# Attention keys projected turned, with their rotary on DVE and GpSimd and partner rows moved by DMA

## The chip, the cores and the metric

One core of a Trainium2 chip. The engines are PE (TensorE, matrix products), ACT (ScalarE), DVE (VectorE), POOL (GpSimd) and SP (it only issues DMAs here). The metric is the device time of one call of the whole layer in microseconds; lower is better.

## What is computed

One decoder layer over a sequence of 512 rows of width 1024, everything in fp32:

```python
u = rms_norm(h, norm_gain);  z = u @ w_in          # 512 x 4420 columns
q_a, k_a, v_a, g_a, q_i, k_i, w_i, q_r, k_r, v_r, g_r = split(z)
q_a, k_a, q_i, k_i = rotary(..., first 16 of 64 head dims, theta 500000)
score = sum_h w_i[t,h] * relu(q_i[t,h] . k_i[s]);  keep the top 128 causal keys
y_a = softmax(q_a k_a^T over the kept keys) v_a * silu(g_a)      # 8 heads x 64
y_r = retention(rotary(q_r), rotary(k_r), v_r) * silu(g_r)       # 4 heads
out = rms_norm(h + concat(y_a, y_r) @ w_out) * final_gain
```

The rotary turns head dims 0 to 7 against their partners 8 to 15: x1 cos - x2 sin and x2 cos + x1 sin. The other 48 dims of a head stay as they are.

## The kernel before, in words

Each fp32 operand of a projection is split into two fp32r parts: ACT writes the rounded part (`w_hi`, L736), DVE the rest (`w_lo`, L1150), and three products (hi·hi, lo·hi, hi·lo) stand for one. The weights come in units of 256 rows by 512 columns (512 KB), four units to a chunk of 512 columns. A unit lives in a ring of six split slots. The chunks are, in order: 0 index, 1 queries, 2 keys, 3 values, 4 retention q and k, 5 retention v, 6 attention gate, 7 retention gate, and then two chunks of `w_out`.

All engines walk through the same list of **slots** g. A chunk has four slots, one for each tile of 128 rows: slot 8 to 11 are the keys, 12 to 15 the values, 16 to 19 retention q/k. In slot g, PE computes 24 products of 512 columns for tile g (`proj`, L527 to L529), with some other work between the first twelve ("first half") and the last twelve ("second half"). Unit u of a chunk is wanted a quarter slot after the one before it; `proj` waits for its `w_lo` at each quarter. Chunk 6 is computed turned: the weights are stationary and 512 tokens move (L523 to L525). The other chunks have x stationary and give tokens by columns.

The order of each engine within a slot is written out by hand, and each engine runs its instructions strictly in order:

- Weight splits (`splits_at`, L143): in slot 4c the first unit of the next chunk, in 4c+1 the second, in 4c+3 the last two. Units 18 and 19, which the second half of slot 16 wants, are so split in slot 15, by ACT and then by DVE.
- Keys: in the slot's end ACT copies the product to `zt`, scaled by the rms factor (L791). POOL turns the first 16 dims of each head in place (L1087, L1088, L1091: five instructions a tile). Two slots later PE transposes the tile in four pieces (L547) into the bank `mid_ps`, ACT writes its rounded part to `k_stack` rows 0 to 63 (L826, two instructions) and DVE the rest to rows 64 to 127 (`key_lo`, L1224, two instructions, one input in PSUM and one in SBUF). Retention q/k (slots 16 to 19) go the same way, with a rotary over all dims.
- `turn_rstd` (PE, slot 15) turns the rms factors into a row for all partitions, `half_rstd_row`, which holds half of each factor.
- Index scores and top-k: in slots 6 to 8 DVE forms the scores of blocks 1 to 3 of 128 queries. Then each block takes 16 rounds of MAX8 (L1261) and MATCH_REPLACE8 (L1263) over 256, 384 or 512 columns, and a mask (L1267) after its last round. `rounds_at` (L175) says how many rounds DVE does at the end of each slot: 4 in slots 6 to 9, 3 in 10 to 15, then 2 until the 48 are done (slot 22).
- `block_q_lo(0)` (DVE, slot 13, L1234): four instructions on 64x512 that split the queries of block 0.
- Attention visits: `scores(0)` is at the end of slot 17 on PE and needs all of `k_stack` (`klo_done`). DVE adds the mask and takes the maxima (L1280), ACT takes exponentials (L866) and scales (L873), PE transposes at the end of slot 18 (L610). Blocks 1, 2 and 3 need their masks from slot 21, 24 and 28.
- POOL in slots 16 to 19: the retention rotary of each tile, which PE transposes two slots later.

Of the kernel before, what the change touches and what calls it, by code (L numbers as in the profile page):

```python
# [12 lines left out]
P = 128  # L13
# [39 lines left out]
LEFT = 5 * P  # L53
C_V, C_RQK, C_RV, C_AG, C_RG = 3, 4, 5, 6, 7
ATT0 = MT * C_RQK
# [65 lines left out]


def first_chunk(x, norm_gain, w_in):
# [51 lines left out]
def rounds_at(slot):  # L175

    done = 0
    for g in range(TOPK0, slot + 1):
        n = min(4 if g <= 9 else 3 if g <= 15 else 2, ROUNDS * (MT - 1) - done)
        done += n  # L180
    return range(done - n, done) if slot >= TOPK0 else range(0)


def transposed(g):

    c = g // MT
    if g < 0 or g >= GROUPS or c not in (0, 1, 2, C_RQK):
        return None
    return g if c < 3 else g - MT


def hymba_layer(nc, x, w_in, w_out, final_gain, table, first, out):
    with ExitStack() as ctx:
# [50 lines left out]
        mix = sb("mix", [P, MT, 2 * ATT_W])  # L244
        attT = mix[:, :, 0:ATT_W]
        first_in = [t[:, :, :].rearrange("p m c -> p (m c)") for t in (mix, x_h)]
        gain = first_in[0][:, 0:NORM]
# [32 lines left out]
        def sems(names):  # L280
# [26 lines left out]
            "idx_lo_done idx_mm relu_done score_step round_step mask_done")  # L307

        klo_done, q_hi_done, q_rest_done, q_lo_done, qk_done, max_done, negmax_done, exp_done = sems(
            "klo_done q_hi_done q_rest_done q_lo_done qk_done max_done negmax_done exp_done")  # L310
# [71 lines left out]
        def _(sp):  # L382
# [51 lines left out]
        def _(pe):  # L434
# [55 lines left out]
            def proj(g, q):  # L490
# [44 lines left out]
            def transpose_group(g):  # L535
# [4 lines left out]
                if i > MT:  # L540
                    pe.wait_ge(t_evac, i)
                if i == 3 * MT:
# [30 lines left out]
            def turn_rstd():  # L573

                pe.wait_ge(rstd_spread, 1)
                pe.wait_ge(t_evac, 3 * MT)
                pe.wait_ge(klo_done, MT)
                for m in range(MT):
# [107 lines left out]
            for g in range(MT, GROUPS + OUT_GROUPS):  # L686
# [37 lines left out]
        def _(act):  # L724
# [41 lines left out]
            def project_out(g):  # L766
# [19 lines left out]
                if i is not None:  # L786
                    if i >= MT + 2:
                        act.wait_ge(t_done, i - 1)
                    if i >= 3 * MT + 2:
                        act.wait_ge(kz_done, i - 3 * MT - 1)  # L790
                    act.activation(zt[:, g % 2, :], src[:, :], ACT.Copy, scale=scale).then_inc(z_done, 1)  # L791
                elif c in (C_V, C_RV):
                    dst = (v_att if c == C_V else v_ret)[:, m, :]
                    act.activation(dst, src[:, :], ACT.Copy, scale=scale).then_inc(z_done, 1)
                else:
                    i = g - MT * C_AG
                    if i > MT:
                        act.wait_ge(rgate_done, i - MT)
                    elif i:
                        act.wait_ge(agate_done, i)  # L800
                    else:
                        act.wait_ge(rope_done, 4 * MT)
                    if i < MT:
# [5 lines left out]
            def transposed_out(g):  # L809
# [6 lines left out]
                if c == 0:  # L816
# [6 lines left out]
                    return  # L823
                if c == 2:
                    for hh in range(2):
                        ins = act.activation(k_stack[0:64, hh::2, t], mid_ps[64 * hh:64 * hh + 64, :].rearrange(  # L826
                            "p (a t) -> p a t", a=PAIRS), ACT.Copy)
                    ins.then_inc(t_evac, 1)
                    return
                if i == 3 * MT:  # L830
                    act.wait_ge(idx_mm, IDX_HEADS * (MT - 1))
                src = mid_ps[:, :].rearrange("p (a t) -> p a t", a=4)
                dst = {1: qT, C_RQK: retT[:, 0:4, :]}[c][:, :, t]
                act.activation(dst, src, ACT.Copy).then_inc(t_evac, 1)

            def relus(b):
# [102 lines left out]
            for g in range(MT, GROUPS + OUT_GROUPS):  # L939
# [11 lines left out]
                if MT + 2 <= g <= 2 * MT:  # L951
                    relus(g - MT - 1)
                if g == ATT0 - 1:
                    rstd_row()
                if g < GROUPS:
                    project_out(g)
# [44 lines left out]
        def _(pool):  # L1001
            step = 0

            def xi_times_q(m):

                t = slice(m * P, (m + 1) * P)
                pool.wait_ge(t_evac, 3 * MT + m + 1)
                pool.tensor_tensor(qxT[:, :, t], qrT[:, :, t], T("xi").rearrange("p (a t) -> p a t", a=2),
# [45 lines left out]
            x_rstd(0)  # L1054
            x_rstd(1)

            for g in range(MT, GROUPS):
# [15 lines left out]
                if ret:  # L1073
                    pool.wait_ge(tab_in, 16)
                if i == 3 * MT:
                    pool.wait_ge(warmed, 1)
                    pool.wait_ge(hrstd_done, 2)
                    pool.tensor_copy(half_rstd_row[:, :].rearrange("p (m t) -> p m t", m=MT), half_rstd.rearrange(
                        "p (m t) -> p m t", t=1).broadcast_to([P, MT, P])).then_inc(rstd_spread, 1)
                zg = g + 1  # L1080
                pool.wait_ge(z_done, zg)
                pool.wait_ge(rope_done, i)
                for s in range(2):

                    if i == 4 * MT - 1 and s:
                        pool.wait_ge(q_lo_done, 2)
# [5 lines left out]
                add.then_inc(rope_done, 1)  # L1092
                if c in (1, 2):
                    continue
# [24 lines left out]
            pad_q(0)  # L1119
            pool.wait_ge(t_done, 4 * MT)  # L1120
            pool.memset(zt[:, :, :], 0.0).then_inc(state_zeroed, 1)
# [25 lines left out]
        def _(dve):  # L1147
# [70 lines left out]

            def key_lo(m):

                t = slice(m * P, (m + 1) * P)
                dve.wait_ge(t_evac, 2 * MT + m + 1)
                for hh in range(2):
                    ins = dve.tensor_tensor(k_stack[64:128, hh::2, t], mid_ps[64 * hh:64 * hh + 64, :].rearrange(  # L1224
                        "p (a t) -> p a t", a=PAIRS), k_stack[0:64, hh::2, t].bitcast(F32), ALU.subtract)
                ins.then_inc(klo_done, 1)

# [190 lines left out]
            for g in range(MT, GROUPS + OUT_GROUPS):  # L1418
# [66 lines left out]
```

## Time and the profile before

| | |
|---|---|
| time, median of 3 runs | 280.89 us (280.73 to 304.37) |
| the profiled execution, its own time | 280.87 us |
| its span in the profile | 279.1 us |
| around the span | 1.77 us |
| busy share: PE, DVE, ACT, POOL | 97%, 72%, 56%, 23% |

The span is the time from the first to the last instruction in the profile of one execution. Times in the rows below are microseconds from its start. The busy share of PE is an upper bound, as its products overlap in the record: how close it is to its limit is read from the distance between the starts of two products.

### The profile page before, as it was taken

The page shows a single profiled execution, that of the slowest core. Times are in us where ns is not written, and L with a number is a line of the kernel's source. Part 1 is how long each engine was busy: PE and PEld are TensorE (multiplying, and loading weights), DVE is VectorE, ACT ScalarE, POOL GpSimd, SP SyncE. Part 2 cuts the span into 40 slices and gives each one's busy share as a digit, 9 for nine tenths or more (in the row PEclk, how much of TensorE's full clock was granted, in tenths as well). Part 3 has the DMA queues.
Part 4 walks back from the last instruction along what each step waited for, and adds up shares of the span by engine and source line. Part 5 has one row for each costly group of instructions (what it writes and reads, how often), then busy time and mean ns, then how long its engine had stood idle before and what let it go on. Part 6 is the DMA issues. An engine that isn't in the chain of part 4 may idle for free.

```text
span 279.1 us, 4372 instructions
## 1 busy us (share of the span) xinstructions
PE 271.7 (97%) x1493; PEld 227.0 (81%) x1493; DVE 200.5 (72%) x419; ACT 157.2 (56%) x331; POOL 64.2 (23%) x116
## 2 busy tenths in 40 slices
PE   8999999999999999999999999999999999999992
PEld 8988888888878788787888888788788888888891
DVE  3786889999999997999696663685656825563342
ACT  4896755536455423767658646776675694241231
POOL 2036622322300059767300102103020020000211
PEclk9999999999999999999999999999999999999999
DMA  7999504220422045052204220040120275111223
GB/s 267 403 400 350 154 4 150 75 76 2 150 76 78 0 150 150 2 150 73 80 2 150 75 78 0 6 147 23 59 73 0 77 237 177 36 41 38 78 88 139
DMA packets 13989, 30.10 MB, mean 108 GB/s; under 512 B 1168, under 2 KB 1680, under 8 KB 13968
## 3 DMA queue, kind: packets, MB, share of 16 engines
q1 hardware_dynamic: 13392, 29.04, 31.2%
q10 hardware_dynamic: 576, 0.79, 0.7%
q8 instruction: 12, 0.20, 0.3%
q14 instruction: 9, 0.07, 0.1%
HBM read 27.73 MB, written 2.10 MB: 107 GB/s over the span
## 4 chain that ended last, share of the span: by engine, by line
PE 67%; DVE 24%; DMA 3%; issue 2%; ACT 2%; SPq 1%; POOLq 0%; DVEq 0%; ACTq 0%
PE bank L527 14%; PE bank L529 13%; PE bank L528 13%; DVE keys L1263 6%; DVE top L1261 6%; DVE w_lo L1150 5%; PE bank L594 4%; PE bank L610 3%; PE bank L523 3%; DMA x_h<-in_first 3%; PE bank L524 3%; PE bank L525 3%; DVE k_stack L1224 2%; PE bank L626 2%; PE bank L625 2%
## 5 line engine op out<-in xcount | busy, mean ns | idle before, releaser
L527 PE MATMUL bank<-w_hi,xT_hi 128*128 128x512 f32 (+1 forms) x264 | 104.2, 395 | 0.1
L529 PE MATMUL bank<-w_hi,xT_lo 128*128 128x512 f32 (+1 forms) x264 | 101.5, 384 | 0.0
L528 PE MATMUL bank<-w_lo,xT_hi 128*128 128x512 f32 (+1 forms) x264 | 101.2, 383 | 0.0
L529 PEld LDWEIGHTS bank<-w_hi,xT_lo 128*128 128x128 f32 x264 | 49.6, 188 | 10.2
L527 PEld LDWEIGHTS bank<-w_hi,xT_hi 128*128 128x128 f32 x264 | 49.7, 188 | 9.8 <-issue 0.7
L528 PEld LDWEIGHTS bank<-w_lo,xT_hi 128*128 128x128 f32 x264 | 49.7, 188 | 8.8
L1150 DVE TENSOR_TENSOR w_lo<-w_raw,w_hi 128x1024 fp32r<-128x1024 f32 x35 | 43.9, 1276 | 13.1 <-ACT w_hi L736 12.8
L736 ACT ACTIVATE w_hi<-w_raw 128x1024 fp32r<-128x1024 f32 x35 | 36.6, 1055 | 6.9 <-PE bank L529 5.0
L1261 DVE MAX8 top<-keys 128x8 f32<-128x256 f32 (+2 forms) x48 | 26.8, 558 | 1.3
L1087 POOL TENSOR_TENSOR th<-zt,tab 128x64 f32<-128x64 f32 (+1 forms) x24 | 12.8, 535 | 62.2 <-ACT zt L791 57.7
L1263 DVE MATCH_REPLACE8 keys<-top,keys 128x256 f32<-128x256 f32 (+2 forms) x48 | 26.0, 542 | 0.0
L791 ACT ACTIVATE zt<-bank,small 128x512 f32<-128x512 f32 x12 | 8.2, 686 | 19.9 <-PE bank L529 19.8
L1021 POOL TENSOR_SCALAR small<-small 128x4 f32<-128x4 f32 (+1 forms) x6 | 1.6, 272 | 57.6 <-ACT st_sb L907 57.1
L866 ACT ACTIVATE work<-work,small 128x128 f32<-128x128 f32 (+3 forms) x16 | 8.8, 554 | 10.2 <-DVE small L1284 10.2
L1400 DVE TENSOR_TENSOR retT<-bank,retT 128x512 f32<-128x512 f32 (+1 forms) x9 | 5.7, 630 | 11.8 <-PE bank L529 11.8
L989 ACT ACTIVATE st_sb<-retT 128x512 f32<-128x512 f32 (+1 forms) x8 | 4.8, 606 | 16.3 <-DVE retT L1400 16.3
L1088 POOL TENSOR_TENSOR tmp<-zt,tab 128x64 f32<-128x64 f32 (+1 forms) x24 | 13.5, 562 | 0.0
L523 PE MATMUL bank<-xT_hi,w_hi 128*128 128x512 f32 x32 | 13.2, 411 | 0.0
L524 PE MATMUL bank<-xT_hi,w_lo 128*128 128x512 f32 x32 | 12.6, 392 | 0.0
L525 PE MATMUL bank<-xT_lo,w_hi 128*128 128x512 f32 x32 | 12.5, 391 | 0.0
L866 ACT ACTIVATE prob_odd<-prob_odd,small 128x128 f32<-128x128 f32 (+3 forms) x16 | 8.8, 553 | 6.4 <-DVE small L1284 6.3
L1116 POOL COPY q_pad<-retT 64x256 f32<-64x256 f32 x8 | 4.3, 535 | 26.8 <-PE bank L635 26.4
(173 smaller groups left out, 442.2 us busy)
## 6 DMA issues: line engine op xcount, KB each, us to landing
w_raw<-in_w_in SPq DMA_DIRECT2D x27, 512.0 KB, 3.8
w_raw<-in_w_out SPq DMA_DIRECT2D x8, 512.0 KB, 3.6
retT<-in_x SPq DMA_DIRECT2D x8, 256.0 KB, 3.4
x_h<-in_first SPq DMA_DIRECT2D x2, 836.0 KB, 8.2
out<-x_h SPq DMA_DIRECT2D x4, 320.0 KB, 2.5
mix<-in_first SPq DMA_DIRECT2D x3, 418.0 KB, 5.3
v_ret<-in_x SPq DMA_DIRECT2D x2, 512.0 KB, 10.4
v_att<-in_x SPq DMA_DIRECT2D x2, 512.0 KB, 12.1
```

Of the source, the lines that this page charges most:

```text
L523: pe.matmul(o, hi[:, kk, e], xT_hi[:, k, :], start=first, stop=False)
L524: pe.matmul(o, lo[:, kk, e], xT_hi[:, k, :], start=False, stop=False)
L525: mm = pe.matmul(o, hi[:, kk, e], xT_lo[:, k, :], start=False, stop=last)
L527: pe.matmul(o, xh, hi[:, kk, c0:c0 + w], start=first, stop=False)
L528: pe.matmul(o, xh, lo[:, kk, c0:c0 + w], start=False, stop=False)
L529: mm = pe.matmul(o, xl, hi[:, kk, c0:c0 + w], start=False, stop=last)
L736: act.activation(split_unit(w_hi, u), raw_unit(u), ACT.Copy).then_inc(whi_done, 1)
L866: act.activation(pr, pr, ACT.Exp, bias=neg_max[:, i:i + 1], scale=HD ** -0.5, accum_out=den[:, b % 2, h:h + 1]).then_inc(exp_done, 1)
L1088: last = chain(pool.tensor_tensor(tb[:, :, s, :], z[:, :, 1 - s, :], sin[:, :, s, :].broadcast_to([P, heads, half]), ALU.mult))
L1150: dve.tensor_tensor(split_unit(w_lo, u), raw_unit(u), split_unit(w_hi, u).bitcast(F32), ALU.subtract).then_inc(wlo_done, 1)
L1261: dve.max(top8[:, :], keys[b][:, :]).then_inc(round_step, 1)
L1263: dve.match_replace(keys[b][:, :], top8[:, :], keys[b][:, :], TAKEN).then_inc(round_step, 1)
```

## The change

The key chunk is computed turned, as chunk 6 already is. ACT then copies each product, unscaled, to `keys_raw` (the storage of `v_ret`): partitions are two heads of 64 dims, columns are tokens. There are no transposes of the key tiles any more. The rotary is done once for all keys, on whole rows of 2048 columns (4 head pairs by 512 tokens):

- SP loads a new 512 KB table (cosines and signed sines by partition and token) into `prob_odd` after unit 10. POOL multiplies both halves by `half_rstd_row` (two instructions on 128x512). `turn_rstd` moves from slot 15 to slot 10 for that, and POOL's spreading of the factors to before its loop.
- Slot 12: ACT issues four DMAs that copy the 8-partition groups of `keys_raw` to their partners' places in `keys_swapped` (the storage of `retT`, 80 partitions by 2048 columns, zeroed by POOL before).
- POOL multiplies `keys_swapped` by the sines: one instruction on 80x2048.
- Slot 13: DVE multiplies `keys_raw` by the cosines, four instructions on 128x512, once the DMAs have landed.
- POOL adds `keys_swapped` to `keys_raw`: one instruction on 80x2048 (`key_roped`).
- Slots 15 and 16: ACT writes the rounded part (`key_hi`, two instructions on 64x1024 in each). Slots 16 and 17: DVE writes the rest (`key_lo`, likewise, now with both inputs in SBUF).
- `rounds_at`: 4 rounds in slots 6 to 8, 3 in 9 to 12, then 2 (until slot 24).

```diff
-        n = min(4 if g <= 9 else 3 if g <= 15 else 2, ROUNDS * (MT - 1) - done)
+        n = min(4 if g <= 8 else 3 if g <= 12 else 2, ROUNDS * (MT - 1) - done)
...
+                if u == APART + RAW:
+                    sp.wait_ge(wlo_done, APART + 1)
+                    sp.dma_start(prob_odd[:, :, :].rearrange("p a t -> p (a t)"), key_table).then_inc(key_table_in, 16)
...
-                    if c == C_AG:
+                    if c in (C_K, C_AG):
...
-                if 2 * MT < i <= 3 * MT:
-                    pe.wait_ge(klo_done, i - 2 * MT)
...
-                if g == ATT0 - 1:
+                if g == MT * C_K + 2:
                     turn_rstd()
...
+                elif c == C_K:
+                    if m == 0:
+                        act.wait_ge(sq_act, 3)
+                        act.wait_ge(sq_dve, 1)
+                    act.activation(keys_raw[:, m, :], src[:, :], ACT.Copy).then_inc(z_done, 1)
...
+            def swap_keys():
+
+                act.wait_ge(z_done, SWAP_AT)
+                act.wait_ge(swapped_zeroed, 1)
+                for hh in range(2):
+                    for x in range(2):
...
+                        act.dma_start(keys_swapped[to, :, :], keys_raw[of, :, :]).then_inc(swapped_in, 16)
+
+            def key_hi(hh):
+
+                act.wait_ge(key_roped, 1)
+                for half in range(2):
+                    act.activation(k_stack[0:64, hh + 4 * half:hh + 4 * half + 3:2, :],
+                                   keys_raw[64 * hh:64 * hh + 64, 2 * half:2 * half + 2, :], ACT.Copy).then_inc(khi_done, 1)
...
+            def rope_keys():
+
+                pool.wait_ge(key_table_in, 16)
+                pool.wait_ge(rstd_row_done, 1)
+                for t in (key_cos, key_sin):
+                    pool.tensor_tensor(t, t, half_rstd_row[:, :], ALU.mult).then_inc(key_table_done, 1)
+                pool.wait_ge(key_table_done, 2)
+                pool.wait_ge(idx_mm, IDX_HEADS * (MT - 1))
+                pool.memset(keys_swapped, 0.0).then_inc(swapped_zeroed, 1)
+                pool.wait_ge(swapped_in, 16 * 4)
+                sin = key_sin[0:TURNED, :].rearrange("p (a t) -> p a t", a=1).broadcast_to([TURNED, PAIRS, SEQ])
+                pool.tensor_tensor(keys_swapped, keys_swapped, sin, ALU.mult).then_inc(key_sined, 1)
+                pool.wait_ge(key_cosed, PAIRS)
+                pool.wait_ge(key_sined, 1)
+                z = keys_raw[0:TURNED, :, :]
+                pool.tensor_tensor(z, z, keys_swapped, ALU.add).then_inc(key_roped, 1)
...
+            def key_cosine():
+
+                dve.wait_ge(key_table_done, 1)
+                dve.wait_ge(swapped_in, 16 * 4)
+                for n in range(PAIRS):
+                    dve.tensor_tensor(keys_raw[:, n, :], keys_raw[:, n, :], key_cos, ALU.mult).then_inc(key_cosed, 1)
+
+            def key_lo(hh):
+
+                for half in range(2):
+                    heads = slice(hh + 4 * half, hh + 4 * half + 3, 2)
+                    dve.wait_ge(khi_done, 2 * hh + half + 1)
+                    dve.tensor_tensor(k_stack[64:128, heads, :], keys_raw[64 * hh:64 * hh + 64, 2 * half:2 * half + 2, :],
+                                      k_stack[0:64, heads, :].bitcast(F32), ALU.subtract).then_inc(klo_done, 1)
...
-                if 0 <= g - 2 - 2 * MT < MT:
-                    key_lo(g - 2 - 2 * MT)
+                if g == SWAP_AT + 1:
+                    key_cosine()
+                if g - SWAP_AT - 4 in (0, 1):
+                    key_lo(g - SWAP_AT - 4)
```

`SWAP_AT` is 12. `retT` is free for retention again once `key_roped` is there (ACT waits for it in slot 18).

## Rows read from the trace of the kernel before

**Rows 1.** The page: busy time by engine, and the granted clock in 40 slices

```profile
PE 271.7 (97%) x1493; PEld 227.0 (81%) x1493; DVE 200.5 (72%) x419; ACT 157.2 (56%) x331; POOL 64.2 (23%) x116
...
PEclk9999999999999999999999999999999999999999
```

**Rows 2.** Waits (engine, line, releaser: us, times, longest): PE on a split

```profile
PEld bank L527 <- DVE w_lo L1150: 0.5, 1, 0.5
```

**Rows 3.** Timeline of PE (start, us, line, xcount): slots 10, 11, 14, 15 begin

```profile
58.53 0.39 PE L527 MATMUL bank<-w_hi,xT_hi 128*128 128x512 f32 x1
...
64.44 0.39 PE L527 MATMUL bank<-w_hi,xT_hi 128*128 128x512 f32 x1
...
82.39 0.39 PE L527 MATMUL bank<-w_hi,xT_hi 128*128 128x512 f32 x1
...
87.83 0.39 PE L527 MATMUL bank<-w_hi,xT_hi 128*128 128x512 f32 x1
```

**Rows 4.** Timeline of PE: middle of slot 16, scores, end of slot 18

```profile
96.25 0.39 PE L529 MATMUL bank<-w_hi,xT_lo 128*128 128x512 f32 x1
96.73 0.50 PE L527 MATMUL bank<-w_hi,xT_hi 128*128 128x512 f32 x1
...
105.03 0.22 PE L625 MATMUL bank<-k_stack,q_hl 128*128 128x128 f32 x1
...
105.88 0.45 PE L527 MATMUL bank<-w_hi,xT_hi 128*128 128x512 f32 x1
...
111.68 0.39 PE L529 MATMUL bank<-w_hi,xT_lo 128*128 128x512 f32 x1
112.22 1.02 PE L610 MATMUL bank<-ident_t,work 128*128 128x128 f32 x4 [0.15 <-ACT work L873]
113.00 0.47 PE L527 MATMUL bank<-w_hi,xT_hi 128*128 128x512 f32 x1
```

**Rows 5.** Timeline of DVE: slot 10, slot 15

```profile
63.88 1.39 DVE L1224 TENSOR_TENSOR k_stack<-bank,k_stack 64x512 fp32r<-64x512 f32 x2
65.30 0.56 DVE L1261 MAX8 top<-keys 128x8 f32<-128x384 f32 x1
...
66.56 0.56 DVE L1261 MAX8 top<-keys 128x8 f32<-128x384 f32 x1
...
95.46 2.35 DVE L1150 TENSOR_TENSOR w_lo<-w_raw,w_hi 128x1024 fp32r<-128x1024 f32 x2
97.72 0.55 DVE L1261 MAX8 top<-keys 128x8 f32<-128x384 f32 x1
```

**Rows 6.** Timeline of ACT: splits of unit 15 and of slot 12

```profile
67.42 1.06 ACT L736 ACTIVATE w_hi<-w_raw 128x1024 fp32r<-128x1024 f32 x1 [0.30 <-PE bank L529]
...
71.16 1.05 ACT L736 ACTIVATE w_hi<-w_raw 128x1024 fp32r<-128x1024 f32 x1
```

**Rows 7.** ACT's line 997, a DMA issue: ns min/median/max, and its landing

```profile
L997 ACTq DMA_DIRECT2D out<-x_h x4: 338/346/376, 260.3 to 276.0; - x4
...
DMA to landing us min/median/max: 2.6/2.8/4.6
```

**Rows 8.** Timeline of POOL: retention rotary of slots 16 and 18

```profile
101.96 0.74 POOL L1087 TENSOR_TENSOR th<-zt,tab 128x256 f32<-128x256 f32 x1
102.66 1.72 POOL L1088 TENSOR_TENSOR tmp<-zt,tab 128x256 f32<-128x256 f32 x1
...
116.85 1.30 POOL L1091 TENSOR_TENSOR zt<-th,tmp 128x512 f32<-128x512 f32 x1
118.23 1.48 POOL L1097 TENSOR_TENSOR kz<-zt,tab 128x256 f32<-128x256 f32 x1
```

**Rows 9.** Timeline of DVE beside POOL: splits, and a round between them

```profile
102.15 1.64 DVE L1150 TENSOR_TENSOR w_lo<-w_raw,w_hi 128x1024 fp32r<-128x1024 f32 x1
103.71 0.68 DVE L1261 MAX8 top<-keys 128x8 f32<-128x512 f32 x1
...
117.29 3.49 DVE L1150 TENSOR_TENSOR w_lo<-w_raw,w_hi 128x1024 fp32r<-128x1024 f32 x2
```

More of the change, by code:

```diff
@@ L120, in tables, with key_tables @@
     return t
+def key_tables():
+    t = np.zeros((2, 2, HD, SEQ), np.float32)
+    inv = np.float32(1.0) / (np.float32(ROPE_THETA) ** (np.arange(ROPE_HALF, dtype=np.float32) / np.float32(ROPE_HALF)))
+    ang = (inv[:, None] * np.arange(SEQ, dtype=np.float32)[None, :]).astype(np.float32).astype(np.float64)
+    t[0] = 2.0
+    for x, sign in ((0, -2.0), (1, 2.0)):
+        t[0, :, x * ROPE_HALF:(x + 1) * ROPE_HALF] = 2.0 * np.cos(ang)
+        t[1, :, x * ROPE_HALF:(x + 1) * ROPE_HALF] = sign * np.sin(ang)
+    return np.ascontiguousarray(t.reshape(2, P, SEQ).transpose(1, 0, 2).reshape(P, 2 * SEQ))
 def first_chunk(x, norm_gain, w_in):
@@ L186, in transposed, with hymba_layer @@
     c = g // MT
-    if g < 0 or g >= GROUPS or c not in (0, 1, 2, C_RQK):
+    if g < 0 or g >= GROUPS or c not in (0, 1, C_RQK):
         return None
-    return g if c < 3 else g - MT
-def hymba_layer(nc, x, w_in, w_out, final_gain, table, first, out):
+    return g if c < 2 else g - 2 * MT
+def hymba_layer(nc, x, w_in, w_out, final_gain, table, first, key_table, out):
     with ExitStack() as ctx:
@@ L575, in turn_rstd @@
                 pe.wait_ge(rstd_spread, 1)
-                pe.wait_ge(t_evac, 3 * MT)
-                pe.wait_ge(klo_done, MT)
+                pe.wait_ge(t_evac, 2 * MT)
                 for m in range(MT):
@@ L788, in project_out @@
                         act.wait_ge(t_done, i - 1)
-                    if i >= 3 * MT + 2:
-                        act.wait_ge(kz_done, i - 3 * MT - 1)
+                    if i >= 2 * MT + 2:
+                        act.wait_ge(kz_done, i - 2 * MT - 1)
                     act.activation(zt[:, g % 2, :], src[:, :], ACT.Copy, scale=scale).then_inc(z_done, 1)
+                elif c == C_K:
[3 more added lines that the diff above has]
+                    act.activation(keys_raw[:, m, :], src[:, :], ACT.Copy).then_inc(z_done, 1)
                 elif c in (C_V, C_RV):
+                    if c == C_RV and m == 0:
+                        act.wait_ge(klo_done, 4)
                     dst = (v_att if c == C_V else v_ret)[:, m, :]
@@ L823, in transposed_out @@
                     return
[L824 to L831, printed above, removed]
+                if i == 2 * MT:
+                    act.wait_ge(key_roped, 1)
                 src = mid_ps[:, :].rearrange("p (a t) -> p a t", a=4)
@@ L834, in transposed_out @@
                 act.activation(dst, src, ACT.Copy).then_inc(t_evac, 1)
+            def swap_keys():
[3 more added lines that the diff above has]
+                    for x in range(2):
+                        here, there = rope_halves(x)
+                        to = slice(HD * hh + here.start, HD * hh + here.stop)
+                        of = slice(HD * hh + there.start, HD * hh + there.stop)
+                        act.dma_start(keys_swapped[to, :, :], keys_raw[of, :, :]).then_inc(swapped_in, 16)
+            def key_hi(hh):
+                act.wait_ge(key_roped, 1)
+                for half in range(2):
+                    act.activation(k_stack[0:64, hh + 4 * half:hh + 4 * half + 3:2, :],
+                                   keys_raw[64 * hh:64 * hh + 64, 2 * half:2 * half + 2, :], ACT.Copy).then_inc(khi_done, 1)
             def relus(b):
@@ L952, in _ @@
                     relus(g - MT - 1)
-                if g == ATT0 - 1:
+                if g == MT * C_K + 2:
                     rstd_row()
+                if g == SWAP_AT:
+                    swap_keys()
+                if g - SWAP_AT - 3 in (0, 1):
+                    key_hi(g - SWAP_AT - 3)
                 if g < GROUPS:
@@ L1083, in _ @@
                 for s in range(2):
-                    if i == 4 * MT - 1 and s:
+                    if i == 3 * MT - 1 and s:
                         pool.wait_ge(q_lo_done, 2)
```

40 lines of the change are left out of this document (21 added, 19 removed).

## The prediction

> **What bounds the kernel now.** I read the page's busy shares first: PE 97%, DVE 72%, and the clock row full in all 40 slices [rows 1]. Then the waits: PE's longest wait on a weight split is one of 0.5 us [rows 2]. Then PE's timeline, slot by slot. Slot 14, which has nothing but its 24 products, takes 87.83 - 82.39 = 5.44 us; slot 10, which also has a key transpose, takes 64.44 - 58.53 = 5.91 [rows 3]. A product starts each 0.227 us (5.44 / 24), so PE is at its limit, and time is won only by giving it less to do or closing its few gaps. The reader is to see two gaps: 96.25 to 96.73, 0.25 us over a product, where unit 18's `w_lo` is late, and 111.68 to 112.22, 0.31 over, where the first probabilities are late [rows 4]. Both come from DVE, which is the second bound: unit 18's split starts at 95.46 and ends about 96.6 [rows 5], just when the second half of slot 16 wants it. A delay on DVE in slots 13 to 17 is therefore a delay of the end.
>
> **What PE loses in work.** Four key transposes go, 0.47 us each (5.91 - 5.44, rows 3): 1.9 us. `turn_rstd` is the same four pieces and only moves. The turned products have the same count and columns. If nothing waited, the new PE timeline would be: slot 10 at 58.53 as before and 5.91 long, slots 11 to 15 at 5.44 each, slot 16 at 91.64, its second half at 94.36, slot 17 at 97.08, `scores(0)` at 102.52. With the two gaps closed as well that is 1.9 + 0.25 + 0.31 = 2.4 us less, 278.4. That is the most the change can win by these rows.
>
> **What DVE gets.** Unit costs, start to start: a round over 384 columns 66.56 - 65.30 = 1.25 us; a split (97.72 - 95.46) / 2 = 1.13; an old `key_lo` 1.42 [rows 5]. A two-input instruction of 512 columns is taken at 0.70 (1.39 / 2, the old `key_lo`), one of 1024 at the split's 1.13. At 63.88 the old DVE has ended round 16 and its mask; the new one is there too: round 16 has left slot 9 and is the first of slot 10's three, with no `key_lo` yet [rows 5]. From there, by the new order:
> - slot 10: two more rounds, 66.4;
> - slot 11: ACT ends unit 15's `w_hi` at 68.4, as before (67.42 + 1.0, rows 6), so unit 15's split ends at 69.55; three rounds, 73.3;
> - slot 12: a split and three rounds, 78.2;
> - slot 13: a split 1.13, four cosines 2.8, `block_q_lo` 2.8, two rounds 2.5; slot 14: two rounds 2.5; slot 15: the split of unit 18, 1.13. Bare, unit 18 is ready at 91.1, over 3 us early.
>
> **The shared lock.** That is without POOL, and here I see the cost. The split at 102.15 takes 1.64 in place of 1.22: POOL's instruction began at 101.96 and took 0.74, to 102.70, and 1.13 from there is the split's end. POOL's next, asked at 102.66, takes 1.72, which is the rest of the split plus its own 0.74 [rows 8, 9]. The pair of splits at 117.29 takes 3.49 against 2.35: the first waits for POOL's 1.30 us add from 116.85 to 118.15, then POOL's next (118.23, 1.48) goes in between, then the second [rows 5, 8, 9]. MAX8 at 103.71, beside a busy POOL, is not slowed. So two-input instructions of DVE and POOL exclude each other whole, and the one that waits gets in after the one that runs.
>
> The Trainium skill has this as a rule (SBUF — State Buffer, Who interferes with whom): a DVE instruction with two SBUF inputs and a GpSimd instruction that reads SBUF hold a shared port for the whole instruction, and the other fully blocks. The trace agrees up to 1.30 us; by the rule it would hold for longer ones also. The old `key_lo` escaped, as one of its inputs was in PSUM; the new one, the cosines and the splits don't.
>
> POOL's two new instructions have 2048 columns. From 256 columns in 0.74 to 512 in 1.30 is 0.56 per 256 [rows 8]; six more steps give 1.30 + 6 x 0.56 = 4.7 us each (bounds: 4 x 1.30 = 5.2 above, the same slope from a start at zero, 4.5, below).
>
> **When they run.** Slot 11 now ends 0.5 us earlier, so ACT's split of slot 12 is at about 70.7 in place of 71.16 [rows 6] and done at 71.75. Four DMA issues of 0.35 follow, the last begins at 72.8, and landing takes 2.6 to 4.6 from the issue [rows 7] (it is 64 KB between partitions, the row is 192 KB to memory, so I take 3.3, between): 76.1. POOL's sine instruction runs 76.1 to 80.8. DVE asks for the split of slot 13 at 78.2 and gets it at 80.8: 2.6 lost; it ends at 81.9, the cosines at 84.7. POOL now asks for its add. DVE does one part of `block_q_lo`, POOL goes in for 4.7, and the other three end at 92.2: 4.7 lost. Four rounds, 97.2. Unit 18 is ready at **98.4**; PE wanted it at 94.36. First stall: 4.0 us.
>
> **The second stall.** PE ends slot 16 at 98.4 + 2.7 = 101.1 and wants `scores(0)` at 106.6. DVE: unit 19, 99.5; two rounds, 102.0; slot 16: a split and two `key_lo` of 1.13, 105.4; POOL has begun the retention rotary of slot 16 at about 102 and slips two 0.74 instructions between them, 106.8; two rounds and a mask, 109.6; slot 17: a split and two `key_lo`, 113.0, and POOL again slips in, with one rest and two whole instructions, 1.9: **114.9**. Only then does PE start the scores, whose 16 products take 105.88 - 105.03 = 0.85 [rows 4]. Slot 18 starts at 115.7, before it was 105.88: 9.8 us late. The gap of 0.31 at the end of slot 18 closes, as DVE takes the maxima at once. In all +9.5, and 280.87 + 9.5 is 290.4; I say **290.0**. The profiled execution and the median (280.89) are the same within 0.02.
>
> **Edits at no cost.** The table load (512 KB behind unit 10) delays unit 11 by about a microsecond, and that is wanted only in slot 11. POOL's spreading, table products and zeroing are on a POOL busy 23% [rows 1], ahead of the swap and beside DVE's rounds, which don't take the lock; the price if DVE's mask meets them is 0 to 1.3 us. ACT's copies of keys cost as before; its `key_hi` waits for `key_roped` (about 90) behind the splits of slot 15 and ahead of that slot's product at 91.6, so its cover is 1.6 us, and what queues behind is one PSUM bank that PE wants a slot later. POOL's rotary of slot 16 begins long after `key_roped`. The rounds are still complete by slot 24, four slots ahead of block 3's visits.
>
> **Rivals.**
> 1. *The lock is not held through a long instruction.* Every row of it is of at most 1.30 us. If DVE slips in, unit 18 is ready at 91.1 to 93, the first stall is none, and `key_lo` ends at 97.1 - 2.6 - 4.7 relative to my sum: 114.9 - 7.3 - about 1.5 (fewer clashes with the rotary) = 106 against 102.5 wanted. A stall of 3.5, less the 2.4 won and 0.4 less of clashes: 281.5.
> 2. *PE never waits: faster.* The place is `klo_done` at the end of slot 17. If the bare DVE sums are right (91.1 for unit 18, then 2 rounds, 2 splits, 4 `key_lo`, 2 rounds and a mask about 104) and some instruction is shorter than its row by a tenth, DVE is there at 102.5, and the time is 278.4. It decides at 2 us less DVE work over slots 13 to 17. For it: DVE is rid of 4 x 1.42 + 3 rounds ahead of unit 18. Against it: the lock.
> 3. *PE's clock falls in the stalls.* No row has a wait of over 0.5 us on PE, and the clock row is full throughout [rows 1, 2]; waits of 4 and 8 us are new. At worst one slot would run at 1.2 GHz, 5.4 us; the likely size is half of that: 292.7. The Trainium skill (TensorE: Matmul & The Clock Gate, Part 1) has an idle array fall to 1.2 GHz until it has been busy again; no run so far shows it here.
> 4. *The swap is late.* Eight partitions of 8 KB each may come slowly. If the four land after 85 rather than 76, both POOL instructions and the cosines move back by as much, and DVE stands still at the cosines: 297.
>
> **How the numbers follow.** Forecast 0.42 (own range 287 to 292), rival 1 0.25, rival 2 0.14, rival 3 0.12, rival 4 0.07. A measurement of this kernel tells 2% from no change, that is 5.6 us: 275.3 to 286.5. Faster: nothing reaches it but errors, 0.02. Slower: forecast, rivals 3 and 4, 0.60. Same: 0.38. The range runs from rival 2 to beyond rival 3: 278.2 to 293.5.
>
> **What would show it.** Two idle stretches on PE: in the middle of slot 16 released by DVE's `w_lo` (4 us), and ahead of the first scores (8 us) released by DVE's `key_lo`. On POOL two instructions on 80x2048 of about 4.7 us. On DVE a split of about 3.7 us near 78, and one instruction of `block_q_lo` of about 5.4 near 85. Slots 11 to 15 at 5.44 us. If the long DVE instructions are missing, the lock was wrong (rival 1); if they are there and PE doesn't wait, my DVE sum was too full. A fall in the granted clock speaks for rival 3, and a DVE wait on the DMAs ahead of the cosines for rival 4.

## The result, and the profile after

The change makes the kernel slower: 292.08 us (median of 6, 290.57 to 292.93) against 280.81, a ratio of 1.039 [1.036, 1.043]. The ratio is that of the means, without one run of the kernel before that took 304.37 us in a slower state; of the changed kernel's six runs two took 290.6 us, the profiled one among them, and four 292.1 to 292.9, so that some 1.5 us of the median stand in no trace. The profiled execution took 290.62 us with a span of 288.8, 9.7 more than the span before. The forecast was 290.0 with a range of 278.2 to 293.5.

The page of the changed kernel: busy time by engine, then PE and its granted clock in 40 slices, to be read beside [rows 1].

```profile
PE 273.3 (95%) x1477; PEld 228.6 (79%) x1477; DVE 213.0 (74%) x419; ACT 156.0 (54%) x327; POOL 72.3 (25%) x101
...
PE   8999999999999494999999999999999999999992
...
PEclk9999999999999788899999999999999999999999
```

Two slices of PE are at 4 tenths, and the clock row, full before, falls about them. PE lost 16 matmul records of transposes, and DVE works 12.5 us longer. PE's waits (line, releaser: us, times, longest) and its timeline from slot 16 to 19, beside [rows 2 and 4]:

```profile
PEld bank L548 <- DVE w_lo L1209: 4.1, 1, 4.1
...
PE bank L643 <- DVE k_stack L1290: 4.3, 1, 4.3
```

```profile
93.99 0.39 PE L550 MATMUL bank<-w_hi,xT_lo 128*128 128x512 f32 x1
98.09 0.80 PE L548 MATMUL bank<-w_hi,xT_hi 128*128 128x512 f32 x1 [3.71 <-DVE w_lo L1209]
98.68 0.63 PE L549 MATMUL bank<-w_lo,xT_hi 128*128 128x512 f32 x1
99.11 0.63 PE L550 MATMUL bank<-w_hi,xT_lo 128*128 128x512 f32 x1
...
103.38 0.55 PE L548 MATMUL bank<-w_hi,xT_hi 128*128 128x512 f32 x1
...
108.78 0.39 PE L550 MATMUL bank<-w_hi,xT_lo 128*128 128x512 f32 x1
113.47 0.33 PE L643 MATMUL bank<-k_stack,q_hl 128*128 128x128 f32 x1 [4.30 <-DVE k_stack L1290]
...
114.83 0.73 PE L548 MATMUL bank<-w_hi,xT_hi 128*128 128x512 f32 x1
...
122.38 0.47 PE L548 MATMUL bank<-w_hi,xT_hi 128*128 128x512 f32 x1
```

The reader is to see two holes and what follows each. In slot 16 PE stands for 3.87 us (98.09 - 93.99 - 0.23) for unit 18, and at the end of slot 17 for 4.46 (113.47 - 108.78 - 0.23) for the last `key_lo`. Behind each hole the products start 0.43 us apart (98.68 to 99.11) in place of 0.23. The windows view (us; busy and count of PE, PEld, DVE, ACT, POOL; granted clock; DMA share; GB/s) has the clock there:

```profile
98.00:102.00 4.00, 3.91 (x9) 3.14 (x10) 3.90 (x9) 0.00 (x0) 0.00 (x0) 0.50 0.69 216
...
113.40:116.00 2.60, 2.53 (x11) 2.34 (x12) 1.42 (x10) 0.00 (x0) 2.52 (x4) 0.60 0.00 0
```

A granted clock of 0.50 is the lower of its two levels, 1.2 GHz; the 0.60 is a mean over a stretch whose first half microsecond was still at 1.0. Where the time went, by the starts of products of both kernels: the second half of slot 16 takes 5.3 us in place of a bare 2.7, the start of slot 17 0.2 more, the scores 1.36 in place of 0.85, the first half of slot 18 1.2 more. So the account of the 9.7 us is: idle +8.3, slow clock +4.4, four key transposes (1.9) with a gap of 0.2 that slot 13 had -2.1, the old gaps of slots 16, 18 and 20 -1.35, a new one in slot 28 +0.5: +9.75.

The cause is on DVE and POOL. DVE's timeline, then POOL's:

```profile
77.90 4.46 DVE L1209 TENSOR_TENSOR w_lo<-w_raw,w_hi 128x1024 fp32r<-128x1024 f32 x1
82.28 2.49 DVE L1283 TENSOR_TENSOR v_ret<-v_ret,prob_odd 128x512 f32<-128x512 f32 x4
84.80 0.69 DVE L1299 TENSOR_TENSOR q_hl<-qT,q_hl 64x512 fp32r<-64x512 f32 x1
85.49 5.00 DVE L1299 TENSOR_TENSOR q_lh<-qT,q_hl 64x512 fp32r<-64x512 f32 x1
...
96.82 2.35 DVE L1209 TENSOR_TENSOR w_lo<-w_raw,w_hi 128x1024 fp32r<-128x1024 f32 x2
...
107.89 2.31 DVE L1209 TENSOR_TENSOR w_lo<-w_raw,w_hi 128x1024 fp32r<-128x1024 f32 x1
110.24 3.18 DVE L1290 TENSOR_TENSOR k_stack<-v_ret,k_stack 64x1024 fp32r<-64x1024 f32 x2
```

```profile
76.66 4.61 POOL L1113 TENSOR_TENSOR retT<-retT,prob_odd 80x2048 f32<-80x2048 f32 x1 [9.68 <-DMA retT<-v_ret]
84.84 5.11 POOL L1117 TENSOR_TENSOR v_ret<-v_ret,retT 80x2048 f32<-80x2048 f32 x1 [3.57 <-DVE v_ret L1283]
...
110.64 1.70 POOL L1146 TENSOR_TENSOR th<-zt,tab 128x256 f32<-128x256 f32 x1
112.30 1.71 POOL L1147 TENSOR_TENSOR tmp<-zt,tab 128x256 f32<-128x256 f32 x1
```

The split asked at 77.90 ends when POOL's sines have ended (81.27) and 1.1 us more are over: 3.2 us lost over its bare 1.22. POOL's add, asked at 84.84, lets one part of `block_q_lo` end (85.5), then runs 4.5 us, and the second part shows as 5.00 us: 4.3 lost. Unit 18 is so ready at 97.95.

### The profile page after: what moved, and what is told of

Same layout as the page of the kernel before. It is cut to its first block, busy times and chain, and to the rows that moved or that the text cites. A ratio compares the mean times of both kernels' runs of the same rounds, so it can differ in the third digit from the quotient of the medians.

```text
span 288.8 us, 4320 instructions
## 1 busy us (share of the span) xinstructions
PE 273.3 (95%) x1477; PEld 228.6 (79%) x1477; DVE 213.0 (74%) x419; ACT 156.0 (54%) x327; POOL 72.3 (25%) x101
## 3 DMA queue, kind: packets, MB, share of 16 engines
q10 hardware_dynamic: 640, 1.05, 1.1%
## 4 chain that ended last, share of the span: by engine, by line
PE 60%; DVE 20%; DMA 7%; ACT 6%; issue 4%; POOL 1%; SPq 1%; POOLq 0%; ACTq 0%; DVEq 0%
PE bank L548 12%; PE bank L550 12%; PE bank L549 12%; DVE w_lo L1209 5%; DMA w_raw<-in_w_in 4%; PE bank L544 4%; PE bank L546 3%; PE bank L545 3%; DMA x_h<-in_first 3%; DVE keys L1328 3%; DVE top L1326 3%; PE bank L612 3%; PE bank L628 2%; DVE q_lh L1299 2%; DVE k_stack L1290 2%
## 5 line engine op out<-in xcount | busy, mean ns | idle before, releaser
L548 PE MATMUL bank<-w_hi,xT_hi 128*128 128x512 f32 (+1 forms) x232 | 92.8, 400 | 3.7 <-DVE w_lo L1209 3.7
L550 PE MATMUL bank<-w_hi,xT_lo 128*128 128x512 f32 (+1 forms) x232 | 90.2, 389 | 0.0
L549 PE MATMUL bank<-w_lo,xT_hi 128*128 128x512 f32 (+1 forms) x232 | 90.1, 389 | 0.0
L544 PE MATMUL bank<-xT_hi,w_hi 128*128 128x512 f32 x64 | 25.8, 403 | 0.0
L545 PE MATMUL bank<-xT_hi,w_lo 128*128 128x512 f32 x64 | 25.0, 391 | 0.0
L546 PE MATMUL bank<-xT_lo,w_hi 128*128 128x512 f32 x64 | 25.0, 390 | 0.0
L544 PEld LDWEIGHTS bank<-xT_hi,w_hi 128*128 128x128 f32 x64 | 12.0, 188 | 2.8 <-issue 0.5
L546 PEld LDWEIGHTS bank<-xT_lo,w_hi 128*128 128x128 f32 x64 | 12.0, 188 | 2.7
L643 PE MATMUL bank<-k_stack,q_hl 128*128 128x128 f32 (+3 forms) x32 | 10.0, 329 | 4.3 <-DVE k_stack L1290 4.3
L545 PEld LDWEIGHTS bank<-xT_hi,w_lo 128*128 128x128 f32 x64 | 12.0, 188 | 2.3
```

Source lines behind the costliest of these rows:

```text
L544: pe.matmul(o, hi[:, kk, e], xT_hi[:, k, :], start=first, stop=False)
L545: pe.matmul(o, lo[:, kk, e], xT_hi[:, k, :], start=False, stop=False)
L546: mm = pe.matmul(o, hi[:, kk, e], xT_lo[:, k, :], start=False, stop=last)
L548: pe.matmul(o, xh, hi[:, kk, c0:c0 + w], start=first, stop=False)
L549: pe.matmul(o, xh, lo[:, kk, c0:c0 + w], start=False, stop=False)
L550: mm = pe.matmul(o, xl, hi[:, kk, c0:c0 + w], start=False, stop=last)
```

## The experiments

All ratios are to the kernel before.

**POOL busy, but reading nothing.** The two long instructions become three memsets each; the keys lack the sine part of their rotary.

```diff
-                pool.tensor_tensor(keys_swapped, keys_swapped, sin, ALU.mult).then_inc(key_sined, 1)
+                for i in range(3):
+                    pool.memset(keys_swapped, 0.0).then_inc(key_sined, 1)
+                    pool.wait_ge(key_sined, i + 1)
...
-                pool.tensor_tensor(z, z, keys_swapped, ALU.add).then_inc(key_roped, 1)
+                for i in range(3):
+                    ins = pool.memset(keys_swapped, 0.0).then_inc(key_sined, 1)
+                    pool.wait_ge(key_sined, i + 4)
+                pool.memset(ms_eps, 0.0).then_inc(key_roped, 1)
```

> The changed kernel with POOL's sine multiplication and its add each replaced by three memsets of the same rows, one after the other (the keys so lack the sine part of their rotary). A memset of 80x2048 took 1.81 us in the changed kernel, so POOL is busy some 5.5 us in place of 4.61 and 5.11, at the same places, but reads nothing. Theory (the lock, taken by what reads): DVE's split near 78 takes 1.2 in place of 4.46 and block_q_lo's second part 0.7 in place of 5.00; unit 18 is ready near 91.6 and the first stall is gone; the last key_lo ends near 105 to 106 against 102.4 wanted, one stall of about 3.5 remains: 282.5 us (281 to 284). Rival (what costs is the length of the key chain through the DMAs and POOL): the chain is no shorter, 292.

285.66 us, 1.017 [1.015, 1.020]. POOL's timeline, then DVE's at the same places:

```profile
76.67 5.54 POOL L1114 MEMSET retT<- 80x2048 f32 x3 [9.73 <-DMA retT<-v_ret]
82.27 5.54 POOL L1120 MEMSET retT<- 80x2048 f32 x3
```

```profile
77.86 1.22 DVE L1214 TENSOR_TENSOR w_lo<-w_raw,w_hi 128x1024 fp32r<-128x1024 f32 x1
...
83.35 0.68 DVE L1304 TENSOR_TENSOR q_lh<-qT,q_hl 64x512 fp32r<-64x512 f32 x1
84.04 0.69 DVE L1304 TENSOR_TENSOR q_hl<-qT,q_lh 64x512 fp32r<-64x512 f32 x1
```

POOL is busy for longer, and DVE's two stretched instructions have their bare lengths. The first stall is gone: unit 18's split now starts at 90.4. So the hold is a matter of POOL reading, and not of the length of the key chain. The time missed the expected one by 3.2 us, since the last `key_lo` ended near 107, not 105 to 106: POOL's retention rotary held up the split ahead of it and both its parts. PE so waited 4.5 us there, and the granted clock from 107 to 112 was 0.50, which the expectation had left out.

**The same work in pieces.** Both long instructions are cut in four of 512 columns (one per head pair).

```diff
-                pool.tensor_tensor(keys_swapped, keys_swapped, sin, ALU.mult).then_inc(key_sined, 1)
+                for n in range(PAIRS):
+                    pool.tensor_tensor(keys_swapped[:, n, :], keys_swapped[:, n, :], key_sin[0:TURNED, :],
+                                       ALU.mult).then_inc(key_sined, 1)
...
-                pool.tensor_tensor(z, z, keys_swapped, ALU.add).then_inc(key_roped, 1)
+                for n in range(PAIRS):
+                    z = keys_raw[0:TURNED, n, :]
+                    ins = pool.tensor_tensor(z, z, keys_swapped[:, n, :], ALU.add)
+                ins.then_inc(key_roped, 1)
```

> The changed kernel with both long POOL instructions cut in four of 512 columns. Theory (DVE and POOL exclude each other, and the one that waits goes in next): POOL still slips 8 x 1.3 us of work in between the split, the four cosines and the four parts of block_q_lo, so DVE ends them near 92.5 as in the changed kernel (91.9): 292 us (290.5 to 293). Rival (the length of a single instruction is the harm, short ones slip through): DVE loses 1 to 2 us in place of 7.5, 284 to 286.

290.96 us, 1.037 [1.036, 1.039]: no gain to speak of. DVE's timeline, then POOL's:

```profile
77.65 1.45 DVE L1213 TENSOR_TENSOR w_lo<-w_raw,w_hi 128x1024 fp32r<-128x1024 f32 x1
79.02 5.79 DVE L1287 TENSOR_TENSOR v_ret<-v_ret,prob_odd 128x512 f32<-128x512 f32 x4
84.84 0.69 DVE L1303 TENSOR_TENSOR q_hl<-qT,q_hl 64x512 fp32r<-64x512 f32 x1
85.55 1.68 DVE L1303 TENSOR_TENSOR q_lh<-qT,q_hl 64x512 fp32r<-64x512 f32 x1
```

```profile
76.72 6.94 POOL L1114 TENSOR_TENSOR retT<-retT,prob_odd 80x512 f32<-80x512 f32 x4 [10.00 <-DMA retT<-v_ret]
84.89 6.90 POOL L1120 TENSOR_TENSOR v_ret<-v_ret,retT 80x512 f32<-80x512 f32 x4 [1.23 <-DVE v_ret L1287]
```

The long waits are gone, but now every instruction of DVE has a piece of POOL ahead of it: the four cosines take 5.79 in place of 2.49, three parts of `block_q_lo` 1.7 each. That is 6.5 us lost in place of 7.5. Unit 18's split starts at 95.55, 1.3 us earlier than in the changed kernel, and the second wait of PE is then 5.95 in place of 4.30. Within a row of two-input instructions it is, in this one cut that was tried, the sum of POOL's work that counts and hardly its pieces.

**The clock.** Products into an unused bank keep PE busy in the stalls (`fill(16)` ahead of the wait for unit 18, `fill(28)` ahead of `scores(0)`).

```diff
+            def fill(count):
+
+                for _ in range(count):
+                    pe.matmul(att_ps[:, :], xT_hi[:, 0, 0:P], xT_hi[:, 0, :], start=True, stop=True)
...
+                if (g, q) == (MT * C_RQK, 2):
+                    fill(16)
...
+                if v == 0:
+                    fill(28)
```

> The changed kernel with 16 products of 512 columns into an unused bank ahead of the wait for unit 18 and 28 ahead of the first scores, to keep PE busy in the two stalls (3.9 and 4.5 us in the changed kernel's profile, and the second grows to about 7 once slot 16 and 17 run at full clock). Theory (the fall of the granted clock after the stalls costs time of its own): products stay 0.227 us apart in slots 16 to 18, granted clock 1.0 all through. The 2.4 us won in slot 16 are given back in the longer second wait, as DVE is no earlier; what shows is 0.5 in the scores and 1.2 in slot 18: 290.3 us (289.5 to 291). Rival (the slow products are a consequence of something else, or cost nothing in sum): 292.

289.55 us, 1.032 [1.030, 1.034], 0.7% under the changed kernel. Windows view of this run, at the time at which the changed kernel's clock was 0.50:

```profile
98.00:102.00 4.00, 3.97 (x18) 2.96 (x17) 3.90 (x8) 0.06 (x1) 0.00 (x0) 1.00 0.48 144
```

PE's timeline behind the fillers:

```profile
107.18 6.51 PE L514 MATMUL bank<-xT_hi 128*128 128x512 f32 x28
114.69 0.33 PE L652 MATMUL bank<-k_stack,q_hl 128*128 128x128 f32 x1 [1.00 <-DVE k_stack L1299]
```

The clock is full, and of the 4.4 us of slow products only a part came back. By the starts of the slots, slot 16 is 2.5 us shorter than in the changed kernel, slot 17 is 2.4 longer and slot 18 is 1.2 shorter: 1.3 in all, where the medians are 2.5 apart. PE is at the scores at 107.2 in place of 109.0 and waits for the same `key_lo` (6.4 us of fillers and 1.0 of idling). The fall of the clock costs in full only where no wait follows.

**The order alone.** `block_q_lo(0)` goes from ahead of the four rounds of slots 13 and 14 to behind them.

```diff
-                if block_split_at(g) is not None:
+                if block_split_at(g):
                     block_q_lo(block_split_at(g))
...
                 for r in rounds_at(g):
                     topk_round(r)
+                if g == ATT0 - 2:
+                    block_q_lo(0)
```

> The changed kernel with block_q_lo(0) moved from slot 13, ahead of the four rounds of slots 13 and 14, to behind them; nothing else. Theory: rounds don't take the lock, so POOL's add runs beside them in 4.6 us and DVE loses only the 3.2 at the split: unit 18 is ready near 93.8 against 94.2 wanted, no first stall; the last key_lo ends at 109 to 110, a stall of about 7 ahead of the scores and a fall of the clock after it: 288 us (287 to 289.5). Rival (a DVE that is free of the lock is no earlier, as something else queues it): 292.

287.29 us, 1.024 [1.023, 1.026]. DVE's timeline, then PE's wait:

```profile
82.16 2.48 DVE L1283 TENSOR_TENSOR v_ret<-v_ret,prob_odd 128x512 f32<-128x512 f32 x4
84.57 0.55 DVE L1326 MAX8 top<-keys 128x8 f32<-128x384 f32 x1
...
89.56 0.69 DVE L1299 TENSOR_TENSOR q_hl<-qT,q_hl 64x512 fp32r<-64x512 f32 x1
...
92.38 2.36 DVE L1209 TENSOR_TENSOR w_lo<-w_raw,w_hi 128x1024 fp32r<-128x1024 f32 x2
```

```profile
PE bank L643 <- DVE k_stack L1290: 7.0, 1, 7.0
```

The same instructions in another order give DVE 4.4 us back, as the rounds run beside POOL's add untouched. The first stall is gone; the second grows to 7.0, as expected, since PE is there earlier.

**DVE's load.** The rounds are taken out of slots 13 to 16, with 3 in slots 17 and 18 and then 2 (done in slot 27), or with 3 from slot 17 (done in slot 24), or the order above together with 2 in slots 13 and 14, none in 15 and 16, then 3.

```diff
-        n = min(4 if g <= 8 else 3 if g <= 12 else 2, ROUNDS * (MT - 1) - done)
+        n = min(4 if g <= 8 else 3 if g <= 12 else 0 if g <= 16 else 3 if g <= 18 else 2, ROUNDS * (MT - 1) - done)
...
+        n = min(4 if g <= 8 else 3 if g <= 12 else 0 if g <= 16 else 3, ROUNDS * (MT - 1) - done)
...
+        n = min(4 if g <= 8 else 3 if g <= 12 else 2 if g <= 14 else 0 if g <= 16 else 3, ROUNDS * (MT - 1) - done)
```

> The changed kernel with no top-k rounds in slots 13 to 16, 3 in slots 17 and 18, then 2 until the 48 are done (slot 27). DVE gives up 4 rounds of 1.25 us ahead of unit 18 and 8 ahead of the last key_lo. Theory (DVE's work in slots 13 to 17 sets both stalls): unit 18 ready at 98.0 - 5.0 = 93.0 against 94.2 wanted, no first stall and no fall of the clock; the last key_lo near 104, a stall of 1 to 2; 279.3 us (278.3 to 281). Rival (the key chain's own latency sets the scores' start, however free DVE is): key_roped is at 90, so it couldn't hold the scores before 95, and this rival would need 288 or more. Rival 2: rounds moved behind slot 17 come back as waits of blocks 2 and 3 for their masks: 283 or more, with gaps of PE in slots 24 to 31.

286.91 us, 1.022 [1.021, 1.024].

> The changed kernel with no top-k rounds in slots 13 to 16 and 3 in each slot from 17, so that all are done in slot 24 as in the changed kernel, not in 27 as in the run with 2 from slot 19. Theory (that run won 9.8 us at slot 18 and lost 7 to 8 again in slots 27 to 29, where DVE has both the rounds and the retention): slot 18 starts at 105.0 again, and most of the late gaps go: 280 us (279.2 to 282). Rival (the late gaps are from the denser key chain or the other order of blocks, not from the rounds in slots 25 to 27): 286 again.

286.09 us, 1.020 [1.018, 1.021].

> The changed kernel with block_q_lo(0) behind the rounds of slot 14 and no rounds in slots 15 and 16, then 3 a slot (done in slot 23). Theory (both parts add: 4.3 us of lock and 5.4 us of rounds leave the way to the last key_lo): key_lo ends near 104 against 102.4, slot 18 starts at 105, no gaps later: 279.3 us (278.6 to 280.5), a little under the kernel before (280.6), as the four transposes are gone and one stall of 1.3 is left. Rival: the gain of the transposes is given back in full by key_lo and the cosines, 280.6 or more.

283.64 us, 1.011 [1.010, 1.013].

In all three slot 18 starts at 104.4 to 105.0, as expected, and in all three the expected total was missed, by 4.3 to 7.6 us. In the first its second rival came true: the rounds come back as gaps of PE in later slots. The rival of the second had the number (286) and not the reason, as slots 27 to 29 are free of the gaps and new ones stand earlier. PE's waits of the first:

```profile
PE bank L662 <- DVE st_sb L1409: 3.6, 2, 3.2
PE bank L653 <- DVE mix L1438: 1.5, 1, 1.5
PE bank L643 <- DVE k_stack L1290: 1.3, 1, 1.3
PE bank L672 <- DVE zt L1427: 1.1, 1, 1.1
```

and of the third:

```profile
PE bank L662 <- DVE st_sb L1409: 1.6, 1, 1.6
PE bank L628 <- ACT work L910: 1.2, 1, 1.2
PE bank L643 <- DVE k_stack L1290: 1.1, 1, 1.1
```

With rounds up to slot 27 DVE is late for the retention (L1409 is its decay) and PE's slots 27 to 29 are together 7.4 us longer than in the changed kernel. With 3 rounds a slot the gaps lie earlier: 6.8 us in slots 22, 24 and 25 of the second, 4.7 in slots 20 to 25 of the third, which moves only four rounds. The first has 18 rounds in slots 17 to 24 and no gap in slots 19 to 24; the second has 24 rounds in slots 17 to 24. So DVE takes 18 rounds there for nothing, and in none of these orders did it find room for the 8 rounds, 10 us, that were moved out of slots 13 to 16.

**The new rule of rounds in the kernel before**, nothing else.

> The kernel before with the new rule of rounds alone (4 in slots 6 to 8, 3 in 9 to 12, then 2; done in slot 24). DVE is 3.75 us ahead at unit 18 and up to 6 us at the first maxima, so the two gaps of PE in slots 16 and 18 (0.4 and 0.5 us) close, and the 0.2 of slot 13 may. Theory: 279.5 us (279.2 to 279.9), 0.3% under the kernel before; the part is good by itself. Rival: the two more slots of rounds cost as much later, 280.5.

279.69 us, 0.997 [0.996, 0.998]: as expected. The gaps of slots 16 and 18 are closed. Slot 28 takes 8.63 us in place of 8.15, so the rule costs 0.5 us there. This part of the change is good by itself, by 1.1 us.

**Rounds beside POOL.** On the changed kernel: slot 13 has four rounds, two ahead of its split (beside the sines), two behind the cosines (beside the add, with the two of slot 14); `block_q_lo(0)` behind them; none in slots 15 and 16, 3 in 17 and 18, then 2.

```diff
-        n = min(4 if g <= 8 else 3 if g <= 12 else 2, ROUNDS * (MT - 1) - done)
+        n = min(4 if g <= 8 else 3 if g <= 12 else 4 if g == 13 else 2 if g == 14 else 0 if g <= 16 else 3 if g <= 18 else 2, ROUNDS * (MT - 1) - done)
...
+                early = 2 if g == SWAP_AT + 1 else 0
+                for r in rounds_at(g)[:early]:
+                    topk_round(r)
...
-                for r in rounds_at(g):
+                for r in rounds_at(g)[early:]:
                     topk_round(r)
+                if g == ATT0 - 2:
+                    block_q_lo(0)
```

> The changed kernel with DVE's rounds laid beside POOL's two long instructions: slot 13 has four, two of them ahead of its split (beside the sines), two behind the cosines; slot 14 has two, then block_q_lo(0) (beside the add); none in slots 15 and 16, 3 in 17 and 18, then 2, done in slot 24. Theory: the split of slot 13 ends near 82.4 with two rounds already done, so DVE loses about 1 us to the lock in place of 7.5; 30 rounds are done by slot 14, the last key_lo ends near 103.5 against 102.4, slot 18 starts at 104.9, and the pattern of rounds from slot 17 is that which had no gaps up to slot 24 in the run with rounds later: 279.1 us (278.6 to 279.8), faster than before by 0.5%. Rival: DVE is full up to slot 24 whatever the order, and 1 to 3 us of gaps come in slots 20 to 25: 280.5 to 282.

279.51 us, 0.997 [0.995, 0.998]. DVE's timeline, then POOL's:

```profile
78.01 0.56 DVE L1326 MAX8 top<-keys 128x8 f32<-128x384 f32 x1
79.27 0.56 DVE L1326 MAX8 top<-keys 128x8 f32<-128x384 f32 x1
80.40 2.05 DVE L1209 TENSOR_TENSOR w_lo<-w_raw,w_hi 128x1024 fp32r<-128x1024 f32 x1
```

```profile
84.94 4.62 POOL L1117 TENSOR_TENSOR v_ret<-v_ret,retT 80x2048 f32<-80x2048 f32 x1 [3.57 <-DVE v_ret L1283]
```

DVE loses 0.8 us to POOL in place of 7.5, the clock doesn't fall, and PE waits 1.0 us at the scores. With the same key chain, the 11 us that the changed kernel loses hang on where its rounds and `block_q_lo(0)` stand.

**The last `key_lo` ahead of slot 17's split**, on that version:

```diff
+                if g == ATT0 + 1:
+                    key_lo(1)
                 for u in splits_at(g):
                     split_lo(u)
...
-                if g - SWAP_AT - 4 in (0, 1):
-                    key_lo(g - SWAP_AT - 4)
+                if g == ATT0:
+                    key_lo(0)
```

> The version with the rounds beside POOL's instructions, and in slot 17 DVE does the last key_lo ahead of the split of unit 21 in place of behind it (the split is wanted only in slot 20, and waits 0.3 us for ACT first). Theory: key_lo starts at 98.5, loses about 1 us to POOL's retention rotary and ends at 101.8 against 102.4 wanted, the last stall (1.0 us and some start-up) is gone: 278.4 us (278.1 to 278.9), faster than the kernel before by 0.8%. Rival: the split behind it meets more of POOL and delays the first maxima, so the gap only moves to the end of slot 18: 279.3.

279.22 us, 0.995 [0.994, 0.996], the fastest of all, but 0.8 short of the theory. The wait at the scores is gone and another is there at the end of slot 20 in PE's timeline:

```profile
123.15 0.39 PE L550 MATMUL bank<-w_hi,xT_lo 128*128 128x512 f32 x1
124.25 1.02 PE L628 MATMUL bank<-ident_t,prob_odd 128*128 128x128 f32 x4 [0.71 <-ACT prob_odd L910]
```

The gap went on to the next thing that DVE feeds, two slots further than the rival had it: the chain that led to it runs over DVE from 98.5 to 123.5, but for 1.7 us of ACT's exponentials. DVE is full there, so the hole moves and hardly shrinks.

How much of this is the turned keys? The new rule of rounds alone took 279.69 us, the rounds beside POOL 279.51 next to the same kernel before (280.74), and the ratios of the fastest version and of the rule alone, 0.9938 to 0.9962 and 0.9955 to 0.9980, overlap. So most of what the best version wins is the rule of rounds; that the turned keys win anything by themselves is not shown clear of noise.

## Why the prediction was right

- *What PE loses in work*: 2.1 us measured in slots 11 to 15, 1.9 forecast; slots 11 to 15 take 5.44 us each. The 0.2 is a gap in slot 13 of the kernel before (6.10 us, where its neighbours have 5.91 to 5.94).
- *The lock*: forecast 2.6 and 4.7 us lost on DVE, measured 3.2 and 4.3; POOL's instructions forecast at 4.7, the first took 4.61, the second 4.62 when nothing held it up. The memsets show that the hold needs POOL to read. The first stall is gone without the holds (memsets) and without the second one alone (the order); it is gone too when the four rounds ahead of unit 18 are taken away and the holds stay, so it is the sum of both that makes it.
- *When they run*: the DMA issues on ACT took 0.63 to 1.22 us each, 3.2 in all, where the old row of 0.35 gave 1.4:

```profile
L864 ACTq DMA_DIRECT2D retT<-v_ret x4: 632/634/1221, 70.6 to 73.1; - x4
```

The sines began at 76.66 all the same (76.1 forecast), since the first issue began at 70.6, beside ACT's split of slot 12 (70.43, 1.05 us), and not behind it at 71.75. From the last issue to the sines it took 3.5 us, with 3.3 forecast for the landing. The errors cancel, which is luck.

- *First stall*: unit 18 ready at 97.95 against 98.4, 3.9 us of idling against 4.0.
- *Second stall*: the mechanism was right and two sizes were off. The last `key_lo` ended near 113.4, not 114.9, as POOL's rotary of slot 16 began at 104.4 and not near 102 and left both `key_lo` of slot 16 their bare 2.35 us. Behind it the slow clock, which the sum left out, took 1.7 us more in the scores and in slot 18. These two cancel, which is luck. The idling itself was 4.5 us in place of 8.3, mostly as PE, held up by the slow clock, was there at 109.0 and not at 106.6.
- *Rival 3*, the fall of the clock, had 0.12 and came true together with the forecast. It was wrong to set it beside the forecast as a case of its own: it follows from the same stalls. Its net price by the fillers is 1.3 us by the starts of slots and 2.5 by the medians (2.7 had been put on it). The profiled execution, for which the sum was made, took 290.62 us against the sum's 290.4; the median is 2.1 above the 290.0, just outside the forecast's own range of 287 to 292. Its sentence on waits holds for the rows shown; the kernel before also has a wait of 1.0 us at its start (PE on DVE's L1153).
- *Rival 1* (no hold through a long instruction) fell: 4.6 us whole. *Rival 2* (no wait of PE) is what the reordered versions come near to, at 279.2 to 279.5. (Its sum of about 104 has three splits in it, units 19, 20 and 21, where the text says two.) *Rival 4*, a late swap, fell: DVE never waited for the DMAs.
- *Edits at no cost*: two small prices. The new rule of rounds costs 0.5 us in slot 28, in the changed kernel and in the kernel before with the rule alone. And DVE's mask met POOL's table products and took 0.98 in place of 0.29 us, within the 0 to 1.3 put on it.

What stays open: nothing was run that takes the cosines and the new `key_lo` away by themselves, so their bare share of DVE's load (about 1.6 us more than the old `key_lo`: 2.5 + 4.7 against 5.6, by bare lengths) is argued, not shown. Both good parts, the transposes gone (1.9) and the new rounds (1.1), would add up to 277.8; the best version is at 279.2, and that DVE's load takes the rest is read from where its last gap went, not shown by a run. Why four of the six runs of the changed kernel took 1.5 us more than the profiled one is open.

## What to carry to other kernels

Work that is taken off the bound engine (2 us of transposes here) must not be paid with two-input SBUF instructions on DVE while GpSimd reads SBUF: count up to GpSimd's whole busy time on DVE's side (here 7.5 of 9.2 us), and don't hope for much from cutting it in pieces (6.5 lost). Lay it beside instructions of DVE that don't meet it. Here those were MAX8 and MATCH_REPLACE8, and in the kernel before the old `key_lo` with an input in PSUM (0.68 to 0.70 us each, also beside POOL); that order alone was worth 4.4 us on DVE. And when a chain has room only because two engines are both nearly full, follow a moved piece of work to its new place before calling it free.

## What the runs showed of the hardware that was not expected

- The granted clock fell to 0.50 about both long waits, with products 0.43 us apart, but not at a fixed place. In the first idling (3.9 us) it fell after 2.7 us. Behind the second (4.5 us) it was still at 1.0 when PE started again: the first four scores are 0.11 us apart, the next ones 0.21. With POOL's work in pieces it fell 1.3 us after an idling of 2.9 us had ended. From PE's restart it took 5.3 and 4.0 us in the changed kernel until products were 0.23 us apart again. After 1.2 us of idling (rounds beside POOL) the clock stayed at 1.0.
- An instruction of DVE with one SBUF input was longer beside POOL too: the mask (TENSOR_SCALAR, 128x256) took 0.98 us beside POOL's two table products (2.60 us), and 0.29 in the kernel before. With POOL's work in pieces the mask over 384 columns took 1.03 beside a retention rotary, and 0.36 in the kernel before.
- The Trainium skill (SBUF — State Buffer, Who interferes with whom) says that a DVE instruction with two SBUF inputs contends with a GpSimd instruction that reads SBUF, not with one that only writes it. The memset run agrees: 1.22 and 0.68 us, each beside a row of three memsets (5.54 us together).
- A DMA issue between partitions on ACT's queue took 0.63 us (median) and up to 1.22, against 0.35 for the issues to memory [rows 7].
